# Routing in a two-layer encoder: picks moved behind a copy, a store on another queue, and turned identities ahead of the experts

## The chip, the cores and the metric

The kernel runs on one core of one Trainium2 chip. The metric is the device time of one execution in microseconds (us). TensorE does the matrix products, VectorE and ScalarE the elementwise work, GpSimd gathers and scatters rows by index, and SyncE issues most DMAs.

## The reference

A trunk of two layers over 1024 tokens of width 1024. Each layer is a mixer with an output projection and a residual add, then an RMS norm and a mixture of experts with two-step routing: the best of 4 groups, then the best two of its 8 experts, so 32 experts in all. The change touches only how the routing is scheduled, and the first moments of the experts.

```python
def hier_moe(x, wg, bg, we, be, w1, w3, w2):
    ...
    g_logits = (xt @ wg).astype(f32) + bg.astype(f32)
    g_prob = jax.nn.softmax(g_logits, axis=-1)
    g_idx = jnp.argmax(g_logits, axis=-1)
    ...
    e_logits = jnp.take_along_axis(e_logits, g_idx[:, None, None], axis=1)[:, 0]
    top_p, top_e = lax.top_k(jax.nn.softmax(e_logits, axis=-1), TOP_K)
    top_p = top_p / jnp.sum(top_p, axis=-1, keepdims=True)
    ...
    def expert_block(args):
        xe, e = args
        hid = jax.nn.silu(xe @ w1[e]) * (xe @ w3[e])
        return hid @ w2[e]
...
for layer in range(DEPTH):
    ...
    x = x + y                      # y: mixer output @ w_out
    x = x + hier_moe(rms_norm(x, ffn_norm[layer]), ...)
```

## The kernel before

The program is written out by hand, engine by engine: each stage is a block in which every engine has its own list of instructions, and semaphores (`wait_ge`, `then_inc`) order them. At the end of a block all engines meet; the next block starts when the last one has arrived. Nothing is scheduled by a planner; the order on an engine is the order in the code.

**Products.** Each product of 32-bit numbers is split into a high and a rest part: three matmuls (lines 211 to 213) of 128x128 by 128x512 for each of the eight pieces `k` of the inner dimension.

**The routing stage** is `out_route` (line 702), called once per layer: `"0"` at about 630 to 772 us and `"1"` at about 1780 to 1934 us. It does the output projection, the residual add, the norm, the router and the lists of tokens for each expert. The loop goes over 8 tiles of 128 tokens. On TensorE, tile `j` is: `project(j, 0)` (24 matmuls, half the columns), the turning of the rows of tile `j - 1` (`turn_x`, line 893, eight transposes by a product with the identity), then `project(j, 1)`, in whose middle (`k == 4`) stand the scores of tile `j - 1` (`logits`, line 912, 16 matmuls of 36 columns). The turned rows are copied out of the accumulator by ScalarE (lower half, line 1023) and VectorE (upper half, `move`, line 1124), and the scores wait for both.

**VectorE** has for each tile: rests of the inputs (line 201), `add(j, 0)` (line 1130), `move(j - 1)`, `add(j, 1)`, the norm's scale (`scale_of`, lines 1136 and 1139), the normed rows `xn` (line 1290). Between them stand the picks: `pick_group` and `pick_experts` turn the scores of one or more tiles into the two chosen experts per token, in some 20 small instructions in a row, each waiting for the one ahead. Before, the picks of tiles 0 to 3 stand at the very start of tile 5's round, those of tiles 4 and 5 at the start of tile 7's, tile 6's is cut in two around the last add, and tile 7's follows at the end. `early_slots` (lines 1235 to 1251) turns picks into places in the experts' lists, from sums that TensorE makes (`early_places`, lines 920 and 924).

**The end of the stage** is a chain: the last pick, `mark_slots` (1246 to 1251), TensorE's `list_slots` (line 941, a pair of matmuls per tile), the slots (line 1306), the gates (1309 to 1318), sixteen matmuls (line 979) and the copy of `slot_gate` (1330, 1331). SyncE stores the last normed rows to `xn_scratch` (line 832), behind two loads of 2 MB of expert weights each (line 179). GpSimd waits for the slots and for that store, and issues the gathers of the first two experts' rows (line 848).

**The experts' stage** is `experts` (line 1951). Per expert: three chunks of weights of 2 MB each, cast to a high part on ScalarE (line 2317) and a rest on VectorE (line 2381) in halves, and the products of lines 2193, 2195 and 2201 on TensorE. It opens on TensorE with `turn_x(0, 0, 0)` (line 2210), eight transposes of the gathered rows. ScalarE first casts one half chunk, then moves the turned rows; VectorE likewise. `idle_products(bank, n)` is an existing helper (line 203) that turns the identity `n` times into an unused bank; other stages open with 36, 30 and 44 of them.

## Time and profile before

| what | value |
|---|---|
| time, median of 3 runs | 2561.81 us (2560.67 to 2567.5) |
| the profiled execution's own time | 2555.0 us |
| its span | 2553.1 us |
| TensorE busy | 2394.8 us (94%) |
| VectorE busy | 1841.6 us (72%) |
| ScalarE busy | 1458.3 us (57%) |
| mean granted TensorE clock | 0.970 |
| routing stage of layer 0, of layer 1 | about 639 to 772, 1780 to 1934 us |

The page gives busy times by engine and, in 40 slices of the span, busy tenths, the granted clock of TensorE (1.0 is 2.4 GHz, 0.5 is 1.2 GHz) and the DMA engines' share. A timeline row is the start in us from the start of the span, the duration, the engine, the line of the kernel, what is written from what, the shape and the count; in square brackets stand the idle time ahead of it and what ended that. Rows of the same kind that follow one another are merged. Matmuls are pipelined, so a row's duration is longer than the distance to the next.

### The profile page before, as it was taken

Reading aid. Unit: us, or ns where it says so; the run is one execution under the profiler, and the core shown is the slowest. Engines: PE = TensorE matmul, PEld = TensorE weight load, DVE = VectorE, ACT = ScalarE, POOL = GpSimd, SP = SyncE. Lnnn points to the kernel's source line nnn. Section 1 sums busy time; section 2 is a strip of 40 time slices with the busy share of each in tenths; the row PEclk is TensorE's granted clock in tenths of the full one; section 3 lists DMA queues with packets and bytes.
Section 4 is the critical chain, followed back from the end, with each engine's and each line's share of the span. In section 5 each row is a group of like instructions: output and inputs, shape, how many; then the busy total and the mean of one; then the engine's idle time right before and its main releaser. Section 6 shows DMA issues by size and latency. Waiting matters only on the chain. (4 is left out here: it accounts for less than half of the span.)

```text
span 2553.1 us, 32636 instructions
## 1 busy us (share of the span) xinstructions
PE 2394.8 (94%) x11674; PEld 1966.4 (77%) x11674; DVE 1841.6 (72%) x2189; ACT 1458.3 (57%) x1782; POOL 478.3 (19%) x433
## 2 busy tenths in 40 slices
PE   8989999897998999999998999997997999999997
PEld 6768877576887888888886877875876888888884
DVE  6838855667468998898894241378668999898983
ACT  6437843321316878888783241267415788888872
POOL 0001100102001332333320000026001433332321
PEclk9999999999998999999998999999998999999999
DMA  5110002110337999999994022022427999999997
GB/s 183 34 67 1 1 17 70 75 34 9 126 134 272 374 393 383 389 383 380 381 379 158 17 105 94 33 50 84 155 80 274 369 385 377 369 397 379 394 378 278
DMA packets 93944, 540.19 MB, mean 212 GB/s; under 512 B 19212, under 2 KB 31085, under 8 KB 68246
## 3 DMA queue, kind: packets, MB, share of 16 engines
q1 hardware_dynamic: 72390, 500.81, 50.4%
q0 software_dynamic: 19008, 33.61, 5.5%
q10 hardware_dynamic: 2448, 4.46, 0.5%
q8 instruction: 62, 1.02, 0.2%
q14 instruction: 36, 0.29, 0.0%
HBM read 519.37 MB, written 55.08 MB: 225 GB/s over the span
## 5 line engine op out<-in xcount | busy, mean ns | idle before, releaser
L2381 DVE TENSOR_TENSOR wL_rest<-ring,wH 128x2048 fp32r<-128x2048 f32 x384 | 868.0, 2288 | 117.1 <-ACT wH L2317 111.1
L2317 ACT CAST wH<-ring 128x2048 fp32r<-128x2048 f32 x384 | 729.5, 1911 | 157.2 <-DMA ring<-in_moe_w 126.7
L2193 PE MATMUL psum<-wH,xgH 128*128 128x512 f32 x1024 | 407.5, 398 | 11.3 <-DVE xgL L2381 11.2
L2195 PE MATMUL psum<-wH,xgL 128*128 128x512 f32 x1024 | 401.1, 392 | 0.0
L2201 PE MATMUL psum<-wL_rest,xgH 128*128 128x512 f32 x1024 | 275.1, 391 | 0.0
L2193 PEld LDWEIGHTS psum<-wH,xgH 128*128 128x128 f32 x1024 | 193.4, 189 | 52.9 <-DVE xgL L2381 13.6
L2201 PEld LDWEIGHTS psum<-wL_rest,xgH 128*128 128x128 f32 x1024 | 192.9, 188 | 40.6
L2195 PEld LDWEIGHTS psum<-wH,xgL 128*128 128x128 f32 x1024 | 193.7, 189 | 38.3
L2193 PE MATMUL psum<-wH,hidH 128*128 128x512 f32 x512 | 206.0, 402 | 3.9 <-DVE hidL L2381 3.9
L2195 PE MATMUL psum<-wH,hidL 128*128 128x512 f32 x512 | 200.2, 391 | 0.0
L2110 POOL COPY gidx<-slots 128x1 int32 (+1 forms) x60 | 61.5, 1025 | 495.6 <-PE psum L2210 495.6
L2201 PE MATMUL psum<-wL_rest,hidH 128*128 128x512 f32 x512 | 137.7, 391 | 0.0
L213 PE MATMUL psum<-xn_high,ring_rest 128*128 128x512 f32 x320 | 126.6, 396 | 0.0
L2193 PEld LDWEIGHTS psum<-wH,hidH 128*128 128x128 f32 x512 | 96.5, 189 | 23.2 <-DVE hidL L2381 4.4
L211 PE MATMUL psum<-w_high_route_rest,y_high_route 128*128 128x512 f32 x256 | 105.4, 412 | 9.3 <-DVE ring_rest L201 8.7
L2201 PEld LDWEIGHTS psum<-wL_rest,hidH 128*128 128x128 f32 x512 | 96.7, 189 | 20.2
L2195 PEld LDWEIGHTS psum<-wH,hidL 128*128 128x128 f32 x512 | 96.7, 189 | 18.3
L2124 POOL COPY yidx<-slots 128x1 int32 (+1 forms) x64 | 97.0, 1516 | 58.0 <-DMA out<-y,yidx 37.9
L213 PE MATMUL psum<-w_high_route_rest,y_rest_route 128*128 128x512 f32 x256 | 101.7, 397 | 0.0
L212 PE MATMUL psum<-ring_rest,y_high_route 128*128 128x512 f32 x256 | 101.2, 395 | 0.0
L2328 ACT ACTIVATE y<-psum,slot_gate 128x1024 f32<-128x1024 f32 x64 | 71.4, 1116 | 51.8 <-PE psum L2201 51.2
L212 PE MATMUL psum<-ring_rest,xn_high 128*128 128x512 f32 x256 | 100.3, 392 | 0.0
(453 smaller groups left out, 4672.5 us busy)
## 6 DMA issues: line engine op xcount, KB each, us to landing
ring<-in_moe_w SPq DMA_DIRECT2D x192, 2048.0 KB
ring<-in_ev_w_in SPq DMA_DIRECT2D x6, 2048.0 KB
ring<-in_od_w_in SPq DMA_DIRECT2D x6, 2048.0 KB
xn_scratch<-xn_route SPq DMA_DIRECT2D x16, 512.0 KB, 2.7
xnT<-in_moe_w SPq DMA_DIRECT2D x4, 2048.0 KB, 12.8
v_att<-in_x SPq DMA_DIRECT2D x8, 512.0 KB, 4.1
ring<-in_ev_w_out SPq DMA_DIRECT2D x2, 2048.0 KB
xnT<-in_x SPq DMA_DIRECT2D x8, 512.0 KB, 3.7
```

Of the source, the lines that this page charges most:

```text
L211: nc.tensor.matmul(dst, lhs[0], rhs[0], start=start, stop=False)
L212: nc.tensor.matmul(dst, lhs[0], rhs[1], start=False, stop=False)
L213: return nc.tensor.matmul(dst, lhs[1], rhs[0], start=False, stop=stop)
L2110: nc.gpsimd.tensor_copy(idx[:, b:b + 1], slots[:, bass.ds(e, 1)]).then_inc(idx_ok, 1)
L2124: nc.gpsimd.tensor_copy(yidx[:, b:b + 1], slots[:, bass.ds(e, 1)]).then_inc(yidx_ok, 1)
L2193: nc.tensor.matmul(psum[:, bank, :], xh[:, k, :], w3[0][:, n, cols], start=(half == 0 and n == 0), stop=False)
L2195: nc.tensor.matmul(psum[:, bank, :], xl[:, k, :], w3[0][:, n, cols], start=False, stop=False)
L2201: ins = nc.tensor.matmul(psum[:, bank, :], xh[:, k, :], w3[1][:, n, cols], start=False, stop=(half == 1 and n == len(ks) - 1))
L2317: nc.scalar.copy(half_of(wH, b, e, c, half), raw(e, c, half)).then_inc(w_high, 1)
L2328: nc.scalar.activation(y[:, b, :], psum[:, 5:7, :].rearrange("p a b -> p (a b)"), ACT.Copy, scale=slot_gate[:, bass.ds(e, 1)]).then_inc(y_ ...
L2381: return nc.vector.tensor_tensor(out, whole, high.bitcast(F32), ALU.subtract)
```

## The change

On **VectorE** the picks of tiles 0 to 3 stand behind `add(5, 0)` and `move(4)`; tile 4's pick stands behind the early lists in tile 6's round; tile 5's opens tile 7's round; tile 6's is whole and stands ahead of the last add. On **TensorE** the scores of tiles 4 and later each wait for a read by the pick three picks back; in the last tile the early sums and tile 6's scores stand at `k == 2`, no longer at 4; the list products of tiles 0 to 3 are put between the two halves of the last turn; the totals (line 973) stand behind the last pair of list products. On **ScalarE** the last `move` stands ahead of the last square, and ScalarE stores the last normed rows from its own queue, ahead of the exponential; SyncE no longer does. In the experts' stage TensorE turns the identity 20 times ahead of `turn_x(0, 0, 0)` and 12 times behind it. No arithmetic of the result changes.

```diff
@@ SyncE
-                            sp.wait_ge(xn_ok, j + 1)
-                            sp.dma_start(xn_d[j * P:(j + 1) * P, :], xn[:, j % 2, :]).then_inc(xn_out[j % 2], 16)
+                            if j < NT - 1:
+                                sp.wait_ge(xn_ok, j + 1)
+                                sp.dma_start(xn_d[j * P:(j + 1) * P, :], xn[:, j % 2, :]).then_inc(xn_out[j % 2], 16)
@@ TensorE, project
-                                if c == 1 and k == 4:
-                                    if j == 7:
+                                if c == 1 and k == (2 if j == NT - 1 else 4) and j:
+                                    if j == NT - 1:
                                         early_places(1)
...
@@ TensorE, logits
-                                if j == 4:
-                                    pe.wait_ge(logit_read, 1)
                                 if j == 5:
                                     pe.wait_ge(places_read, 1)
-                                if j == 6:
-                                    pe.wait_ge(logit_read, 2)
-                                if j == 7:
-                                    pe.wait_ge(logit_read, 3)
+                                if j >= 4:
+                                    pe.wait_ge(logit_read, j - 3)
@@ TensorE, end of the stage
                         turn_x(NT - 1, 0)
+                        pe.wait_ge(marked, 1)
+                        list_slots(0, 4)
                         turn_x(NT - 1, 1)
...
-                        list_slots(0, 6)
+                        list_slots(4, 6)
                         places(7, 0)
                         pe.wait_ge(marked, 3)
                         list_slots(6, 7)
-                        pe.wait_ge(places_read, 3)
+                        pe.wait_ge(marked, 4)
+                        list_slots(7, 8).then_inc(listed, 1)
                         for j in range(NT):
                             last = nc.tensor.matmul(psum[:, 1, 0:NE], onesR[:], both[:, j, :], start=(j == 0), stop=(j == NT - 1))
                         last.then_inc(totalled, 1)
-                        pe.wait_ge(marked, 4)
-                        list_slots(7, 8).then_inc(listed, 1)
@@ ScalarE
+                            if j == NT - 1:
+                                move(j)
                             act.wait_ge(added, 2 * j + 2)
...
-                            if j == NT - 1:
-                                move(j)
...
+                        act.wait_ge(xn_ok, NT)
+                        nc.scalar.dma_start(xn_d[(NT - 1) * P:NT * P, :], xn[:, (NT - 1) % 2, :]
+                                            ).then_inc(xn_out[(NT - 1) % 2], 16)
@@ VectorE
                         for j in range(NT):
-                            if j == 5:
-                                pick_group(slice(0, 4))
-                                pick_experts(slice(0, 4))
                             if j == 7:
-                                pick_group(slice(4, 6))
-                                pick_experts(slice(4, 6))
+                                pick(slice(5, 6))
...
                             if j:
                                 move(j - 1)
+                            if j == 5:
+                                pick(slice(0, 4))
                             if j == 6:
...
                                 early_slots(0)
+                                pick(slice(4, 5))
                             if j == 7:
                                 early_slots(1)
-                                pick_group(slice(6, 7))
+                                pick(slice(6, 7))
                             add(j, 1)
...
-                                pick_experts(slice(6, 7))
@@ experts, TensorE
+                        idle_products(OB, 20)
                         turn_x(0, 0, 0)
+                        idle_products(OB, 12)
```

`pick(js)` is `pick_group(js)` followed by `pick_experts(js)`. `early_places` and `places` wait for the picks by their new count.

On VectorE at tile 5 of layer 0, before (L1231 is the last instruction of the picks of tiles 0 to 3, L1124 the copy of the turned rows, L1130 an add):

```order
L1189 TENSOR_TENSOR chosen<-idx_route,mk_route 128x128
L1231 TENSOR_TENSOR both_route<-chosen 128x128
L201 TENSOR_TENSOR y_rest_route<-yT,y_high_route 128x512 x2
L1130 TENSOR_TENSOR xnT<-xnT,psum 128x512
L1124 COPY xnT<-psum 128x512
L1130 TENSOR_TENSOR xnT<-xnT,psum 128x512
```

and in the change:

```order
L201 TENSOR_TENSOR y_rest_route<-yT,y_high_route 128x512 x2
L1130 TENSOR_TENSOR xnT<-xnT,psum 128x512
L1124 COPY xnT<-psum 128x512
L1202 TENSOR_TENSOR logits_route<-psum,rs_route 128x144
L1207 TENSOR_TENSOR logits_route<-logits_route,b_route 128x144
L1209 TENSOR_REDUCE gm_route<-logits_route 128x4
```

The copy L1124 stood behind the picks and now stands ahead of them; the picks (from L1202 on) now have the second add behind them.

On TensorE at the end of the routing stage of layer 0, before (L893 turns a half of the last rows, L941 lists, L973 totals, L979 weighs; phase_sem1_41 is `marked`, phase_sem1_38 `picked`, phase_sem1_47 `places_read`):

```order
L893 MATMUL psum<-ident,xnT 128x128 [waits phase_sem1_3,phase_sem1_16,phase_sem1_15]
L893 MATMUL psum<-ident,xnT 128x128 x3
L893 MATMUL psum<-ident,xnT 128x128 [waits phase_sem1_3]
L893 MATMUL psum<-ident,xnT 128x128 x3
...
L941 MATMUL psum<-tok_of_route,xnT_rest 128x32 [waits phase_sem1_41]
L941 MATMUL psum<-tok_of_route,xnT_rest 128x32
L973 MATMUL psum<-both_route,ones_route 128x32 [waits phase_sem1_47]
L973 MATMUL psum<-both_route,ones_route 128x32 x7
L941 MATMUL psum<-tok_of_route,xnT_rest 128x32 [waits phase_sem1_41]
L941 MATMUL psum<-tok_of_route,xnT_rest 128x32
L979 MATMUL psum<-w_high_route_rest,xnT_rest 128x64 [waits phase_sem1_40]
```

and in the change (L937 lists, L931 places, L972 totals, L976 weighs):

```order
L893 MATMUL psum<-ident,xnT 128x128 [waits phase_sem1_3,phase_sem1_16,phase_sem1_15]
L893 MATMUL psum<-ident,xnT 128x128 x3
L937 MATMUL psum<-tok_of_route,xnT_rest 128x32 [waits phase_sem1_41]
L937 MATMUL psum<-tok_of_route,xnT_rest 128x32 x7
L893 MATMUL psum<-ident,xnT 128x128 [waits phase_sem1_3]
L893 MATMUL psum<-ident,xnT 128x128 x3
...
L931 MATMUL psum<-both_route,upper_route 128x32 [waits phase_sem1_38]
L937 MATMUL psum<-tok_of_route,xnT_rest 128x32 [waits phase_sem1_41]
L937 MATMUL psum<-tok_of_route,xnT_rest 128x32
L937 MATMUL psum<-tok_of_route,xnT_rest 128x32 [waits phase_sem1_41]
L937 MATMUL psum<-tok_of_route,xnT_rest 128x32
L972 MATMUL psum<-both_route,ones_route 128x32 x8
L976 MATMUL psum<-w_high_route_rest,xnT_rest 128x64 [waits phase_sem1_40]
```

Eight list products now stand between the halves of the turn, and the totals behind the last pair of lists.

On TensorE at the start of the experts of layer 0, before (L2210 turns the gathered rows, L2193 is the first product):

```order
L792 UNCONDITIONAL_BRANCH
L2184 UNCONDITIONAL_BRANCH [waits barrier_Pool_Activation_PE_DVE_SP_release]
L2210 MATMUL psum<-ident,xg 128x128 [waits gather_in0]
L2210 MATMUL psum<-ident,xg 128x128 x7
L2193 MATMUL psum<-wH,xgH 128x512 [waits phase_sem0_5,phase_sem0_4]
```

and in the change (L206 turns the identity, L2211 the gathered rows, L2194 is the first product):

```order
L792 UNCONDITIONAL_BRANCH
L2185 UNCONDITIONAL_BRANCH [waits barrier_Pool_Activation_PE_DVE_SP_release]
L206 MATMUL psum<-ident 128x128 x20
L2211 MATMUL psum<-ident,xg 128x128 [waits gather_in0]
L2211 MATMUL psum<-ident,xg 128x128 x7
L206 MATMUL psum<-ident 128x128 x12
L2194 MATMUL psum<-wH,xgH 128x512 [waits phase_sem0_5,phase_sem0_4]
```

The identity is turned 20 times ahead of the wait for the gather and 12 times ahead of the first product.

## Rows read from the trace of the kernel before

**Rows 1.** Timeline, VectorE and TensorE at tile 5 of both layers (start us, us, engine).

```profile
710.72 0.30 DVE L1202 TENSOR_TENSOR logits_route<-psum,rs_route 128x144 f32<-128x144 f32 x1
...
716.75 1.29 DVE L201 TENSOR_TENSOR y_rest_route<-yT,y_high_route 128x512 fp32r<-128x512 f32 x2
...
719.29 1.08 PE L912 MATMUL psum<-w_gain_route,xnT 128*128 128x36 f32 x8 [2.47 <-DVE xnT L1124]
...
1878.04 1.43 PE L912 MATMUL psum<-w_gain_route,x_turned_route 128*128 128x36 f32 x8 [3.67 <-DVE x_turned_route L1124]
```

**Rows 2.** Timeline at tile 6 of both layers, same columns.

```profile
731.42 1.22 DVE L1251 TENSOR_TENSOR xnT_rest<-place_of,cst 128x1024 fp32r<-128x1024 f32 x1
...
732.57 1.87 PE L912 MATMUL psum<-w_gain_route,xnT 128*128 128x36 f32 x16
...
1893.68 1.23 DVE L1251 TENSOR_TENSOR xnT_rest<-place_of,cst 128x1024 fp32r<-128x1024 f32 x1
...
1893.83 1.87 PE L912 MATMUL psum<-w_gain_route,x_turned_route 128*128 128x36 f32 x16
```

**Rows 3.** Timeline of layer 0 from the last product of the stage.

```profile
751.48 0.60 PE L893 MATMUL psum<-ident,xnT 128*128 128x128 f32 x4
...
757.52 0.26 DVE L1199 SCALAR_TENSOR_TENSOR logits_route<-psum,rs_route,b_route 128x36 f32<-128x36 f32 x1 [0.19 <-PE psum L912]
...
761.29 0.22 DVE L1235 TENSOR_TENSOR tok_of_route<-chosen,tok 128x64 fp32r<-128x64 f32 x1
...
762.78 0.43 DVE L1251 TENSOR_TENSOR xnT_rest<-place_of,cst 128x256 fp32r<-128x256 f32 x1
...
765.19 0.19 DVE L1306 TENSOR_SCALAR slots<-psum 128x32 int32<-128x32 f32 x1 [1.68 <-PE psum L941]
...
771.93 0.19 DVE L1331 TENSOR_TENSOR slot_gate<-slot_gate,psum 128x32 f32<-128x32 f32 x1
```

**Rows 4.** Timeline of layer 1 at the same places.

```profile
1913.15 0.60 PE L893 MATMUL psum<-ident,x_res_route 128*128 128x128 f32 x4
...
1918.92 0.25 DVE L1199 SCALAR_TENSOR_TENSOR logits_route<-psum,rs_route,b_route 128x36 f32<-128x36 f32 x1
...
1934.15 1.90 ACT L2317 CAST wH<-ring 128x2048 fp32r<-128x2048 f32 x1 [8.97 <-PEq L792]
```

**Rows 5.** Chain of waits at the end of layer 1 (start us, us, what).

```profile
1919.03 12.80 DMA xn_scratch<-xn_route
...
1932.90 3.77 DMA xg<-xn_scratch,slots
```

**Rows 6.** DMA issues of the whole span (KB each, median us to landing).

```profile
sigmoid_o_scratch<-ml_sigmoid_o ACTq DMA_DIRECT2D x16, 256.0 KB, 2.0
...
xg<-xn_scratch,oidx POOLq DMA_INDIRECT x3, 6.8
```

**Rows 7.** Timeline, head of layer 0's experts, then layer 1's second expert.

```profile
772.47 1.90 ACT L2317 CAST wH<-ring 128x2048 fp32r<-128x2048 f32 x1 [8.69 <-PEq L792]
...
772.90 1.97 PE L2210 MATMUL psum<-ident,xg 128*128 128x128 f32 x8 [1.24 <-DMA xg<-xn_scratch,slots]
777.95 0.79 PE L2193 MATMUL psum<-wH,xgH 128*128 128x512 f32 x1 [3.08 <-DVE xgL L2381]
...
783.10 0.40 PE L2193 MATMUL psum<-wH,xgH 128*128 128x512 f32 x1
...
788.55 2.29 DVE L2381 TENSOR_TENSOR wL_rest<-ring,wH 128x2048 fp32r<-128x2048 f32 x1 [2.35 <-ACT wH L2317]
...
793.89 0.50 PE L2193 MATMUL psum<-wH,xgH 128*128 128x512 f32 x1 [1.56 <-DVE xgL L2381]
...
1955.24 0.50 PE L2193 MATMUL psum<-wH,xgH 128*128 128x512 f32 x1 [1.56 <-DVE xgL L2381]
```

**Rows 8.** Windows: engines busy, PEclk, DMA share, GB/s; stage start and experts.

```profile
1364.00:1372.00 8.00, 7.52 (x44) 7.48 (x44) 3.50 (x5) 6.50 (x9) 0.00 (x0) 0.62 0.82 272
...
2060.00:2080.00 20.00, 20.00 (x98) 16.66 (x96) 18.14 (x12) 17.08 (x15) 6.21 (x5) 1.00 1.00 391
```

15 lines of the change are left out of this document (8 added, 7 removed).

## The prediction, made before the changed kernel was run

> **What bounds the kernel now.** I read the windows first, then the waits in order of time. In the experts' stages TensorE is busy 20.00 of 20.00 us at full clock and the DMA share is 1.00 [rows 8], so there nothing is idle and a microsecond won at the start of a stage moves everything behind it. The change touches the two routing stages and the start of the two experts' stages behind them; I write "tile" for 128 tokens, E for the moment at which TensorE starts to turn the last tile's rows (751.48 and 1913.15 [rows 3, 4]) and T for ScalarE's first cast of the experts' stage (772.47 and 1934.15 [rows 4, 7]). From S to T it is 20.99 and 21.00 us, and this stretch is a chain through VectorE: last picks, slots, gates, a last product. Inside the routing stage TensorE runs back to back but for one pause per layer, at tile 5: 2.47 and 3.67 us, both ended by VectorE's copy of the turned rows [rows 1]. In the timeline the reader is to see why: VectorE begins the picks of tiles 0 to 3 at 710.72 and reaches its next other work at 716.75 [rows 1], 6.03 us in which the copy waits.
>
> **Step 1, the picks of tiles 0 to 3 behind the copy.** TensorE's pause goes: -2.47 and -3.67. What is late next is VectorE's second add of tile 5. With the copy done about 3.3 us after 710.72, the 6.03 us of picks end some 9.2 us behind it. That product ends a little under 13 us behind 710.72 before; less the pause, that leaves about 1 us of slack in layer 0, and 1.5 us by the same count in layer 1. I take nothing for it.
>
> **Step 2, the new wait.** The scores of tile 5 now wait until VectorE has read the scores of tile 4, and that read is queued behind the early marks. In layer 0 the marks end at 731.42 + 1.22 = 732.64 and TensorE comes at 732.57; with the read's 0.26 (the one-tile read in [rows 3]) and a hand-over that is 0.4 us. In layer 1 they end at 1893.68 + 1.23 = 1894.91 against TensorE at 1893.83 [rows 2]: 1.08 + 0.26 = 1.3 us. Both engines come earlier by the same pause, so the differences stand. Bounds: 0.3 to 0.6 and 1.2 to 1.6. Behind the waiting TensorE stand only its own products of tile 6. Splitting tiles 4 and 5 costs VectorE two picks of 761.29 - 757.52 = 3.77 us [rows 3] in place of one double, in its idle time under the products of tiles 6 and 7; the second ends just as TensorE asks for it, which may cost 0.1.
>
> **Step 3, the last pick starts sooner.** It starts 757.52 - 751.48 = 6.04 us behind S in layer 0 and 1918.92 - 1913.15 = 5.77 in layer 1 [rows 3, 4]. Ahead of it stood the second part of tile 6's pick, 10 of its 16 instructions, so 10/16 x 3.77 = 2.4 us; that is now over before the last add. Not all of it is won, since the copy then waits for the turned rows: eight list products stand between the two halves of the turn, 0.12 us each by the 16 in 1.87 of [rows 2], and TensorE stood idle for part of that already. Turn, copy, mean, root and scaling then follow one another, and I put the start at S + 4.7: -1.3 and -1.1. From 0 to -2.4, nearer the middle because both ends of the chain are known.
>
> **Step 4, the totals behind the lists.** VectorE waits 1.68 us for the lists [rows 3]. Its last mark is ready at 762.78 + 0.43 = 763.21, and the last pair of list products, at the slow clock 1.97 / 8 = 0.25 each [rows 7], needs 0.5; the eight totals stood ahead of them. Without those the slots come 1.3 us sooner: -1.3 per layer (-1.0 to -1.4). The totals fall into TensorE's wait for the gates, and nobody waits for them.
>
> **Step 5, the store from ScalarE's queue.** In layer 1 the last normed rows take 12.80 us to land behind 4 MB of weights on SyncE's queue, and the gather behind them 3.77 [rows 5]. On ScalarE's own queue it can take 2.0 us, the quiet price for half the size, or 6.8, a gather's price while weights stream [rows 6], or still 12.80. ScalarE has nothing to do there but wait for the exponential's input, so the issue costs nothing. I take 6.8: issued at S + 4.6, landed by S + 11.5, when the slots are there too (S + 11.1). Then GpSimd no longer ends the stage; VectorE's chain does, and -0.3 more falls to layer 1, where T came later behind it. The Trainium skill (DMA: Bandwidth & Descriptors, Queues, rings and completion order) has each DMA engine take turns between the queues packet by packet, which speaks for the middle price; no row here shows two such queues at once.
>
> **Sum up to T.** Layer 0: -2.5 + 0.4 - 1.3 - 1.3 = -4.7. Layer 1: -3.7 + 1.3 - 1.1 - 1.3 - 0.3 = -5.1.
>
> **Step 6, the turned identities.** Before, the first twelve products ran from 777.95 to 783.10, 5.15 us, 0.43 us each. The 98 matmuls in 20 us of [rows 8], one in seven of them a short turn, come to 0.22 to 0.23 us for a long one, 2.7 us for twelve: 2.4 us is what the risen clock is worth. The price: 20 turns at the slow clock are at most 20 x 0.25 = 4.9 us by the eight in 1.97 [rows 7], and about 4.3 since the last one's full length is in those 1.97; only then come the eight of x. Turned identities do bring the clock up in this trace: the stage that begins before 1372 opens with 44 of them and nothing else, busy 7.52 of the 8 us from 1364.00, so from 1364.48; the mean granted clock over these 8 us is 0.62 [rows 8], that is 6.1 us at the lower level (1.2 GHz) and the rest at 2.4 GHz, a rise 5.5 us after the first turn. The long products after 777.95 had it within about 5 us (0.79 us for the first, 0.40 at 783.10 [rows 7]). If it rises 4 us behind T, x is turned by T + 5.3 in place of T + 2.4, ScalarE's casts of the weights behind it come 3 us late, and the first product starts at T + 6.8 in place of 777.95 - 772.47 = 5.5, but warm. The first twelve are then over at T + 9.5 in place of T + 10.6. VectorE has 2.35 us of idle time at 788.55 [rows 7] to take up ScalarE's lateness. The second expert starts at T + 20.4 in place of 793.89 - 772.47 = 21.4 in layer 0 and of 1955.24 - 1934.15 = 21.1 in layer 1: -1.0 and -0.7. Bounds: a rise at 5.5 us leaves -0.5 and -0.2, one at 3 us gives -1.8 and -1.5; with the clock up at T already it would be -2.4 each. Weights follow VectorE's casts and land well ahead of their use at the head.
>
> **Total.** -4.7 - 5.1 - 1.0 - 0.7 = -11.5. The profiled execution is 2555.0 us (span 2553.1); the median of the three timed runs is 2561.81, 6.8 above. So 2543.5 in the profile's terms and 2550.3 as a median; I forecast **2550.3**. Its own range, by the bounds above and the 2 us by which runs differ, is 2546 to 2555.
>
> **Rivals.**
> *A, the identities don't raise the clock.* Then 20 turns, eight of x and twelve more stand in a row at the slow clock: first product at T + 8.9, first twelve as slow as before, second expert 3.4 and 3.7 us later than now: -9.8 + 7.1 = -2.7, **2559.1**. Against it speaks the rise at 1364.48 + 5.5 under turned identities alone. The Trainium skill (TensorE: Matmul & The Clock Gate, Part 4: PE-mode transpose) says that the full clock "doesn't engage" for transposes; by that rule A holds, and this trace disagrees with it, with 0.62 over a stretch that holds only turns.
> *B, the store stays late.* If the weights, issued first, still hold it back 11 to 13 us, the gathers start at S + 16 to S + 18 and T is 0.5 and 1.6 later than in my sum; the rows still land ahead of the turned identities' end. -9.4, **2552.4**. For it: all 16 DMA engines are shared; against it: 6.8 for a gather among the same loads.
> *C, slower than before.* The store and the gathers go on ending the stage, so that T stays at S + 21.0 and only the pauses are won (-2.1 and -2.4), and the turned identities then stand in the chain at the slow clock with their whole 7.1: -4.5 + 7.1 = +2.6, **2564.4**. It decides at a landing later than S + 18; before it was 1931.83 - 1913.15 = 18.7 (12.80 behind 1919.03 [rows 5]). Both conditions are needed, and each has a row against it.
> *D, the clock is up early.* If what TensorE does at the end of routing counts too, or the rise comes within 3 us, the head gives up to 4.8 in place of 1.7: **2547.2**. Against it: the same small products left it slow before, through the turns of x at 0.25 us each [rows 7].
> *E, the stall of step 1 reappears.* The picks delay an add that TensorE needs; up to 2 us per layer back: **2554.3**.
>
> **How the numbers follow.** Forecast 0.55, A 0.08, B 0.15, C 0.04, D 0.10, E 0.08. The range goes from D's 2547 less noise to A's 2559: 2545 to 2559; C and the outer part of D stay out. 0.3%, about what a measurement of this kernel can tell from no change, is 7.7 us: faster means under 2554.1. That holds for the forecast but its upper edge, for D, most of B and half of E: 0.75. A, the rest of B and E, and most of C are within: 0.22. Slower by that much needs more than C: 0.03.
>
> **What would show it.** Step 1: the pauses of 2.47 and 3.67 before TensorE's scores at tile 5 are gone. Step 2: short idle times of about 0.4 and 1.3 before its scores at tile 6. Steps 3 and 4: the last pick at S + 4.7 and slots at S + 11.1, from 13.7 before. Step 5: a landing of 5 to 8 us and gathers right behind the slots. Sum: T at S + 18.3. Step 6: granted clock 1.00 from the first product on and the second expert at T + 20.4. Wrong if T stays at S + 21, if the first products take 0.43 us each, or if the experts' stage stretches by what its start won.

## The result, and the profile after

The changed kernel takes 2546.97 us (median of 8 runs, 2543.09 to 2550.17) against 2562.28 us (8 runs, 2554.51 to 2567.5) for the kernel before, measured beside it. The ratio is 0.9940, with a 95% interval of 0.9926 to 0.9954: faster by 15.3 us, 0.6%, clear of the noise. The prediction said 2550.3 with a range of 2545 to 2559, so the median lies 3.3 us below the forecast and inside the range. (Where the prediction introduces "E for the moment at which TensorE starts to turn the last tile's rows", it means the S that all its sums use; so do the texts below.)

The profiled execution took 2544.74 us (span 2542.7), 10.3 us less than the profiled one of before. So the medians differ by 5 us more than the profiles do, and that is the first question for the experiments.

Timeline of the changed kernel at tiles 5 and 6 of both layers (start us, us, engine, line, what, count, idle time ahead). It answers [rows 1, 2]:

```profile
715.84 1.87 PE L908 MATMUL psum<-w_gain_route,xnT 128*128 128x36 f32 x16
...
730.25 1.95 PE L908 MATMUL psum<-w_gain_route,xnT 128*128 128x36 f32 x16 [0.18 <-issue]
...
1867.31 1.87 PE L908 MATMUL psum<-w_gain_route,x_turned_route 128*128 128x36 f32 x16
...
1883.64 1.95 PE L908 MATMUL psum<-w_gain_route,x_turned_route 128*128 128x36 f32 x16 [1.18 <-issue]
```

At tile 5 the 16 products for the scores follow without a pause, in both layers. At tile 6 the new wait stands where step 2 put it. The row prints 0.18 us of it in layer 0; by the distance between two turns of x the tile costs 0.42 more than before (14.49 in place of 14.07). In layer 1 it is 1.18 us.

Timeline from the last turn of x to ScalarE's first cast, against [rows 3, 4]: last turn, last pick, slots, product for the gates, the two gathers, slot gates, then the same two ends in layer 1.

```profile
749.39 0.60 PE L893 MATMUL psum<-ident,xnT 128*128 128x128 f32 x4
...
753.83 0.26 DVE L1199 SCALAR_TENSOR_TENSOR logits_route<-psum,rs_route,b_route 128x36 f32<-128x36 f32 x1
...
760.22 0.19 DVE L1307 TENSOR_SCALAR slots<-psum 128x32 int32<-128x32 f32 x1 [0.39 <-PE psum L937]
...
763.08 3.62 PE L976 MATMUL psum<-w_high_route_rest,xnT_rest 128*128 128x64 f32 x16 [1.19 <-DVE w_high_route_rest L1319]
...
765.70 1.23 POOL L849 DMA_INDIRECT xg<-xn_scratch,slots  x1 [128.47 <-issue]
767.22 1.00 POOL L849 DMA_INDIRECT xg<-xn_scratch,slots  x1 [0.30 <-issue]
...
766.96 0.19 DVE L1332 TENSOR_TENSOR slot_gate<-slot_gate,psum 128x32 f32<-128x32 f32 x1
...
1904.58 0.60 PE L893 MATMUL psum<-ident,x_res_route 128*128 128x128 f32 x4
...
1922.68 1.90 ACT L2320 CAST wH<-ring 128x2048 fp32r<-128x2048 f32 x1 [7.40 <-PEq L792]
```

The last pick starts at S + 4.44, the slots at S + 10.83, the slot gates 0.35 us ahead of T. T is 767.50 = S + 18.11, and in layer 1 S + 18.10 (20.99 and 21.00 before). VectorE's wait for the lists fell from 1.68 to 0.39 us. One thing did not happen: the gathers go out at S + 16.3, not at S + 11, because the store on ScalarE's queue still lands late.

Head of the experts' stage on TensorE, against [rows 7]:

```profile
767.54 4.50 PE L206 MATMUL psum<-ident 128*128 128x128 f32 x20 [0.84 <-PEq L792]
771.83 1.66 PE L2211 MATMUL psum<-ident,xg 128*128 128x128 f32 x8
773.32 1.47 PE L206 MATMUL psum<-ident 128*128 128x128 f32 x12
774.89 0.50 PE L2194 MATMUL psum<-wH,xgH 128*128 128x512 f32 x1
...
788.53 0.50 PE L2194 MATMUL psum<-wH,xgH 128*128 128x512 f32 x1 [1.60 <-DVE xgL L2384]
...
1943.11 0.50 PE L2194 MATMUL psum<-wH,xgH 128*128 128x512 f32 x1 [1.56 <-DVE xgL L2384]
```

The second expert starts at T + 21.03 in layer 0 and T + 20.43 in layer 1, in place of 21.42 and 21.09.

### The profile page after: what moved, and what is told of

Its sections match the earlier page's. It is cut to its first block and busy times, and to the rows that moved or that the text cites. A ratio compares the mean times of both kernels' runs of the same rounds, so it can differ in the third digit from the quotient of the medians.

```text
span 2542.7 us, 32784 instructions
## 1 busy us (share of the span) xinstructions
PE 2399.4 (94%) x11738; PEld 1972.5 (78%) x11738; DVE 1847.5 (73%) x2211; ACT 1461.0 (57%) x1782; POOL 491.3 (19%) x433
## 5 line engine op out<-in xcount | busy, mean ns | idle before, releaser
L2194 PE MATMUL psum<-wH,xgH 128*128 128x512 f32 x1024 | 405.7, 396 | 7.0 <-DVE xgL L2384 6.7
L2194 PEld LDWEIGHTS psum<-wH,xgH 128*128 128x128 f32 x1024 | 192.6, 188 | 47.2 <-DVE xgL L2384 8.9
L2194 PE MATMUL psum<-wH,hidH 128*128 128x512 f32 x512 | 206.0, 402 | 3.9 <-DVE hidL L2384 3.9
L2111 POOL COPY gidx<-slots 128x1 int32 (+1 forms) x60 | 70.5, 1174 | 497.0 <-PE psum L2211 497.0
L2125 POOL COPY yidx<-slots 128x1 int32 (+1 forms) x64 | 111.0, 1735 | 52.7 <-DMA out<-y,yidx 27.2
L2194 PEld LDWEIGHTS psum<-wH,hidH 128*128 128x128 f32 x512 | 96.5, 189 | 23.2 <-DVE hidL L2384 4.4
```

The source lines that it names most:

```text
L2111: nc.gpsimd.tensor_copy(idx[:, b:b + 1], slots[:, bass.ds(e, 1)]).then_inc(idx_ok, 1)
L2125: nc.gpsimd.tensor_copy(yidx[:, b:b + 1], slots[:, bass.ds(e, 1)]).then_inc(yidx_ok, 1)
L2194: nc.tensor.matmul(psum[:, bank, :], xh[:, k, :], w3[0][:, n, cols], start=(half == 0 and n == 0), stop=False)
```

## The experiments

Twelve runs were made: the kernel before once more, and eleven variants. The table holds what their timelines show. "Tile 5" and "tile 6" are the distances from one first turn of x (the row with ident as input and xnT or x_res, x8) to the next, layer 0 / layer 1; T - S, the first weights load behind T and the second expert behind T are read as above. "Lost" is what the experts from the fifth on took above 17.70 us each, from one turn of gathered rows to the next, summed over a stage. Medians are in us; the ratio is to runs of the kernel before on the same chip. These runs were spread over several chips, on which the kernel before had medians of 2560.6 to 2562.7, so two variants are better compared by their ratios.

| kernel | tile 5 | tile 6 | T - S | first load | second expert | lost | median (runs) | ratio to before |
|---|---|---|---|---|---|---|---|---|
| before, first profile | 16.26 / 20.01 | 14.07 / 14.57 | 20.99 / 21.00 | 7.65 / 9.31 | 21.42 / 21.09 | 0.3 / 1.3 | 2562.28 (8) | |
| before, second profile | 19.11 / 21.59 | 14.09 / 14.59 | 20.71 / 21.20 | 7.65 / 9.18 | 20.43 / 21.74 | 0.1 / 3.7 | 2560.06 (8) | 0.9997 |
| picks03 | 13.64 / 14.56 | 14.09 / 14.57 | 20.71 / 21.02 | 7.65 / 9.24 | 21.91 / 22.25 | 1.8 / 6.3 | 2551.77 (6) | 0.9959 |
| changed | 13.61 / 14.56 | 14.49 / 17.52 | 18.11 / 18.10 | 10.76 / 10.09 | 21.03 / 20.43 | 0.5 / 0 | 2546.97 (8) | 0.9940 |
| picks_old | 19.50 / 19.97 | 14.07 / 14.57 | 19.42 / 19.42 | 9.78 / 10.26 | 20.16 / 20.65 | 0.6 / 7.5 | 2557.92 (12) | 0.9987 |
| totals_ahead | 13.64 / 14.56 | 14.47 / 15.97 | 19.38 / 19.38 | 10.19 / 10.88 | 20.52 / 21.14 | 0.3 / 6.5 | 2547.05 (4) | 0.9944 |
| store_sync | 13.64 / 14.56 | 14.47 / 15.95 | 19.62 / 20.22 | 10.07 / 9.97 | 20.44 / 20.33 | 1.7 / 1.1 | 2549.25 (5) | 0.9957 |
| no_ident | 13.61 / 14.56 | 14.48 / 15.97 | 18.11 / 18.11 | 8.25 / 8.90 | 20.55 / 21.43 | 0.7 / 0.3 | 2546.75 (5) | 0.9942 |
| cast_first | 13.61 / 14.56 | 14.47 / 17.51 | 18.11 / 18.12 | 6.46 / 6.45 | 21.32 / 21.34 | 2.2 / 0.9 | 2546.52 (6) | 0.9932 |
| loads_same | 13.61 / 14.56 | 14.47 / 15.98 | 18.11 / 18.11 | 10.62 / 9.96 | 21.00 / 20.35 | 3.0 / 2.4 | 2545.59 (4) | 0.9931 |
| fill | 13.61 / 14.56 | 14.49 / 17.53 | 19.22 / 20.74 | 10.26 / 10.27 | 20.60 / 20.60 | 0 / 1.6 | 2546.82 (5) | 0.9941 |
| best1 | 13.61 / 14.56 | 14.07 / 14.57 | 18.64 / 18.54 | 9.38 / 9.25 | 21.18 / 21.21 | 1.8 / 2.5 | 2547.74 (6) | 0.9954 |
| best0 | 13.61 / 14.56 | 14.07 / 14.57 | 18.67 / 18.10 | 10.70 / 10.05 | 20.98 / 20.40 | 2.9 / 1.8 | 2543.79 (6) | 0.9932 |
| best2 | 13.61 / 14.56 | 14.07 / 14.57 | 18.37 / 17.91 | 10.65 / 9.86 | 21.00 / 20.22 | 0.2 / 4.1 | 2544.40 (6) | 0.9929 |

The intervals of the ratios are 0.001 to 0.002 to either side, 3 to 5 us. What lies within that of the changed kernel's 0.9940 is told apart by the timelines alone, and the last column says no more than "about the same".

### before_again: was the first profile typical?

> The kernel before, unchanged, profiled a second time. What is asked: whether the profile on which the prediction rests was a typical execution. Theory (a pause of TensorE is sometimes followed by a stretch at a granted clock of 0.50 and sometimes not, so the same pause has two prices): tile 5 of layer 0, from one first turn of x to the next, takes 16.26 us again or about 19.5, and in layer 1 20.0 again or 18.2; everything else up to S is as in the first profile within 0.1 us. Rival (the first profile was typical and the 5 us by which the medians differ more than the profiles lie in the experts' stages): both tiles as in the first profile, 16.26 and 20.01, and the experts' stages differ by more than 2 us.

Measured: 2564.55 us in the profiled execution, where the first one of before took 2555.0. Timeline of TensorE, the turns of x of tiles 4 and 5 and the products behind the pause between them; then windows of 2 us (us, busy time of PE, PEld, DVE, ACT and POOL, the granted clock, the DMA share, GB/s):

```profile
711.16 1.04 PE L893 MATMUL psum<-ident,xnT 128*128 128x128 f32 x8
...
718.21 1.92 PE L912 MATMUL psum<-w_gain_route,xnT 128*128 128x36 f32 x8 [2.43 <-DVE xnT L1124]
...
730.27 1.03 PE L893 MATMUL psum<-ident,xnT 128*128 128x128 f32 x8
...
717.00:719.00 2.00, 0.80 (x4) 0.80 (x4) 1.15 (x2) 0.00 (x0) 0.00 (x0) 0.61 0.00 0
719.00:721.00 2.00, 2.00 (x9) 1.81 (x9) 0.00 (x0) 0.00 (x0) 0.00 (x0) 0.50 0.03 8
721.00:723.00 2.00, 2.00 (x6) 1.58 (x5) 0.00 (x0) 0.00 (x0) 0.00 (x0) 0.50 0.00 0
723.00:725.00 2.00, 2.00 (x7) 1.55 (x6) 0.01 (x1) 0.00 (x0) 0.00 (x0) 0.68 0.00 0
```

and the same windows in the first profile of before:

```profile
719.00:721.00 2.00, 1.71 (x12) 1.58 (x13) 0.23 (x1) 0.00 (x0) 0.00 (x0) 1.00 0.04 8
721.00:723.00 2.00, 2.00 (x10) 1.66 (x9) 0.00 (x0) 0.00 (x0) 0.00 (x0) 1.00 0.00 0
```

The same pause, 2.43 us in place of 2.47, cost 5.50 us here (19.11 against the 13.61 of a tile without it) and 2.65 in the first profile. The difference is the granted clock: it fell to 0.50, the 1.2 GHz level, as TensorE stood idle, and TensorE then worked for some 6 us at that level, busy 2.00 of 2.00 us. Six microseconds at half speed lose 3, and 2.4 + 3 is nearly the whole 5.5. In the first profile it stayed at 1.00. In layer 1 the pause of 3.67 us cost 5.45 the first time and 7.03 the second. The theory holds for layer 0; for layer 1 neither expectation had 21.59.

The two profiles of before differ by 9.6 us in all, and tile 5 of both layers is 4.4 of them. Another 3.5 lie ahead of, between and behind the stages that the change touches (-1.1, 2.8 and 1.8), and 1.7 in the experts' stages (-1.3 and 3.0). So the rival is wrong on the tiles and right in part on the rest: the price of the pause is the largest single item of the difference between two executions, not the whole.

### picks03: step 1 alone

```diff
                         for j in range(NT):
-                            if j == 5:
-                                pick_group(slice(0, 4))
-                                pick_experts(slice(0, 4))
...
                                 move(j - 1)
+                            if j == 5:
+                                pick_group(slice(0, 4))
+                                pick_experts(slice(0, 4))
```

> The kernel before with step 1 alone: the picks of tiles 0 to 3 stand behind the copy of the turned rows at tile 5, all else as before. Theory (the pause and the stretch of slow clock behind it are most of the gain): tile 5 takes 13.61 and 14.56 us in place of 16.26 (19.5 with the slow stretch) and 20.01, from the first turn to S 91.1 and 96.2 us, T at S + 21.0 as before; the time is 8 to 11 us below the kernel before's median. Rival (step 1 is worth its two pauses, 2.47 + 3.67, or VectorE's second add of tile 5 is late instead): 4 to 6 us below.

Measured: 2551.77 us against 2560.87, ratio 0.9959 (0.9946 to 0.9973): 9.1 us by the medians and 10.5 by the ratio, from moving one step of VectorE behind one copy. Tiles and S are as the theory said (S 91.10 and 96.22 us behind the first turn), T - S as before.

### picks_old: all but the picks

The picks and TensorE's waits for them stand as before; everything else is the changed kernel. (The edit is the part of the diff on picks, logits and places, backwards.)

> The changed kernel with steps 1 to 3 undone: the picks stand where they stood before (0 to 3 ahead of tile 5's adds, 4 and 5 together ahead of tile 7, tile 6's pick split around the last add), and so do TensorE's waits for them; the list of tiles 0 to 3 between the two halves of the turn, the order of totals and lists, the store and the turned identities stay as changed. Theory (steps 1 to 3 as on record, plus what the clock adds: in layer 1 the pause of 3.67 us is followed by a stretch at a granted clock of 0.50): from the first turn of tile 0 to S 93.7 us in layer 0 and 101.7 in layer 1, where the changed kernel has 91.66 and 99.16; the last pick starts 6.0 and 5.8 us behind S, T comes at S + 19.4. Sum 2.1 + 2.5 + 1.3 + 1.3 = 7.2 us above the changed kernel's time, 8.7 where that one was spared the dip at tile 6. Rival (the gain of the picks is found again elsewhere, the rest of the change carries it): under 4 us above.

Measured: 2557.92 us, 11 above the changed kernel (12 by the ratios); expected were 7.2 to 8.7, by the rival under 4. T - S grew by 1.3 in both layers, as step 3 had it. Tile 5 of layer 0 took more than expected. Its pause on TensorE:

```profile
719.11 1.70 PE L913 MATMUL psum<-w_gain_route,xnT 128*128 128x36 f32 x8 [2.48 <-DVE xnT L1129]
```

The pause is 2.48 us, and between the turns around it lie 19.50: the price with the slow stretch, a second time. Between the two profiles 2.6 us are at the tail; up to S this profile is 5.3 us longer in layer 0 than the changed kernel's and 2.5 in layer 1 (4.0 against the profiles without the slow stretch at tile 6).

### totals_ahead: step 4 undone

```diff
-                        pe.wait_ge(marked, 4)
-                        list_slots(7, 8).then_inc(listed, 1)
+                        pe.wait_ge(places_read, 3)
                         for j in range(NT):
...
                         last.then_inc(totalled, 1)
+                        pe.wait_ge(marked, 4)
+                        list_slots(7, 8).then_inc(listed, 1)
```

> The changed kernel with step 4 undone: the eight totals stand ahead of the last list products. Theory: VectorE waits 1.7 us for the lists in place of 0.39, slots and T come 1.3 us later in each layer (T at S + 19.4), the time is 2.6 us above the changed kernel's. Rival (GpSimd, whose gathers went out only at S + 16.3 and S + 16.8, ends the stage anyway or the product for the gates does): T at S + 18.1 to S + 18.5 and no difference in time over 1 us.

Measured: T at S + 19.38 in both layers, 1.27 later than in the changed kernel, which is step 4 as predicted. Its median of 2547.05 is 0.1 above the changed kernel's, from four runs that range from 2543.22 to 2551.66: the time neither confirms nor refutes 2.6 us.

### store_sync: step 5 undone

```diff
-                            if j < NT - 1:
-                                sp.wait_ge(xn_ok, j + 1)
-                                sp.dma_start(xn_d[j * P:(j + 1) * P, :], xn[:, j % 2, :]).then_inc(xn_out[j % 2], 16)
+                            sp.wait_ge(xn_ok, j + 1)
+                            sp.dma_start(xn_d[j * P:(j + 1) * P, :], xn[:, j % 2, :]).then_inc(xn_out[j % 2], 16)
...
-                        act.wait_ge(xn_ok, NT)
-                        nc.scalar.dma_start(xn_d[(NT - 1) * P:NT * P, :], xn[:, (NT - 1) % 2, :]
-                                            ).then_inc(xn_out[(NT - 1) % 2], 16)
```

> The changed kernel with step 5 undone: the last normed rows are stored from SyncE's queue, behind the 4 MB of weights. Theory (the store is late on either queue, so the queue is worth what VectorE's chain leaves uncovered): the store lands 11 to 13 us behind its issue in place of 10.7 and 11.3, the gathers go out 0 to 1.5 us later, T stays at S + 18.1 in layer 0 and comes up to 1.2 us later in layer 1, 0 to 1.2 us in all. Rival (the store on ScalarE's queue is what lets VectorE's chain end the stage): T at S + 19.5 or later in both layers and 3 us or more in all.

Measured: the store lands 13.4 and 13.8 us behind its issue, T comes at S + 19.62 and S + 20.22, 1.5 and 2.1 us later; the median is 2.3 above the changed kernel's. The rival holds by the marks (3.6 us in both layers; 4.4 by the ratios). With VectorE's chain shortened to S + 18.1, the store on SyncE's queue ends the stage, so its move is worth 3.6 us in this kernel, and not the 0.3 of the prediction. Without it, steps 3 and 4 leave only 1.4 and 0.8 us of the 2.9 per layer.

### loads_same: the store beside the loads, not behind them

```diff
                             if j == NT - 1:
+                                sp.wait_ge(xn_ok, NT)
                                 for c in range(2):
```

> The changed kernel, but the two chunks of weights (4 MB) that are issued at the start of the last tile's turn wait until the last rows are normed, so they are issued at S + 4.5, at the same moment as the store on ScalarE's queue. Theory 1 (the store was held up by the 4 MB issued ahead of it, in the DMA engines themselves): with both issued together the store lands in 2.5 to 5 us in place of 10.7 and 11.3, and the first gather goes out right behind the slots, at S + 11, in place of S + 16.3 and S + 16.8. Theory 2 (the two queues share the engines for as long as both have work, whatever came first): the store still needs 6.8 us or more. For the time: if VectorE's chain ends the routing stage, T stays at S + 18.1 and the time within 1 us of the changed kernel's; if GpSimd's gathers end it, T falls to S + 17 or less.

Measured: issued at the same moment (751.07 and 751.06 us), the store lands in 9.0 and 9.2 us. Theory 2 holds. T stays at S + 18.11 although the gathers go out at S + 14.6 and S + 14.7: VectorE's chain ends the stage in the changed kernel, as the sum had it. This run also shows the price of tile 6 in layer 1 at its other value. First the changed kernel, windows behind its new wait of 1.18 us, which ends at 1883.64 (fields as above):

```profile
1884.00:1886.00 2.00, 2.00 (x17) 1.92 (x17) 1.70 (x9) 0.00 (x0) 0.00 (x0) 0.96 0.00 0
1886.00:1888.00 2.00, 2.00 (x6) 1.55 (x5) 0.99 (x5) 0.00 (x0) 0.00 (x0) 0.50 0.00 0
1888.00:1890.00 2.00, 2.00 (x8) 1.54 (x8) 0.00 (x0) 0.00 (x0) 0.00 (x0) 0.69 0.00 0
```

and loads_same, the row with the same wait and the windows behind it:

```profile
1885.65 1.95 PE L909 MATMUL psum<-w_gain_route,x_turned_route 128*128 128x36 f32 x16 [1.18 <-issue]
...
1886.00:1888.00 2.00, 2.00 (x18) 1.91 (x18) 1.69 (x9) 0.00 (x0) 0.00 (x0) 1.00 0.00 0
1888.00:1890.00 2.00, 2.00 (x10) 1.65 (x9) 1.01 (x5) 0.00 (x0) 0.00 (x0) 1.00 0.00 0
```

The same idle time of 1.18 us, the same work; in one execution TensorE fell to 0.50 behind it and the tile took 17.52 us, in the other it stayed at 1.00 and the tile took 15.98. (By the windows the stretch at 0.50 lasted 3.3 us, of which half, 1.6, is the difference.) Three of the seven kernels with this wait show about 17.5 (changed, cast_first, fill), four show about 16.0.

### no_ident: the head without turned identities

```diff
-                        idle_products(OB, 20)
                         turn_x(0, 0, 0)
-                        idle_products(OB, 12)
```

> The changed kernel without its turned identities (neither the 20 nor the 12); all else stays. Theory of step 6 (the identities raise the clock and what they cost is less than what they give): the first twelve long products take 0.43 us each again, the granted clock is 0.50 until about T + 10, the second expert starts at T + 21.0 to T + 21.4 as before, where the changed kernel had T + 21.03 and T + 20.43, so the time is 0.4 to 1.7 us above the changed kernel's. Rival (the identities only delay the turn of x, ScalarE's casts and with them the first weights load, and give back later what the clock won): the first weights load starts at T + 7.7 to T + 9.3 in place of T + 10.8 and T + 10.1, the third expert of layer 1 takes 19.5 us in place of 21.53, and the time is 1 to 3 us below the changed kernel's.

Measured: 2546.75 us, no difference from 2546.97. The second expert of both layers on TensorE, and the windows in which the granted clock rose (fields as above):

```profile
786.33 0.50 PE L2194 MATMUL psum<-wH,xgH 128*128 128x512 f32 x1 [1.56 <-DVE xgL L2382]
...
1942.46 0.50 PE L2194 MATMUL psum<-wH,xgH 128*128 128x512 f32 x1 [1.56 <-DVE xgL L2382]
...
774.00:776.00 2.00, 2.00 (x9) 1.64 (x8) 2.00 (x2) 1.98 (x2) 0.00 (x0) 0.91 0.66 133
...
1931.00:1933.00 2.00, 2.00 (x9) 1.65 (x8) 2.00 (x2) 1.46 (x2) 0.00 (x0) 0.88 0.76 221
```

T is 765.78 and 1921.03, so the second expert starts at T + 20.55 and T + 21.43: 0.5 us sooner than with the identities in layer 0, 1.0 us later in layer 1. Neither theory has both signs. The clock did what step 6 said: without identities it rises 8.6 and 10.4 us behind T, in the changed kernel 5.6 and 4.1. What that is worth is not settled. Over all profiles, the 16 heads with identities as changed average T + 20.6 (20.16 to 21.14), and the eight heads without (before twice, picks03, no_ident) T + 21.35 (20.43 to 22.25), 0.7 us later; but six of these eight belong to kernels whose end of routing also differs. The two of no_ident alone average T + 20.99, against 20.70 in changed and loads_same: 0.3 us. And where the rows of the 32nd expert are turned, the 16 are at T + 550.3 and T + 552.6 on average and the eight at T + 550.2 and T + 553.0, so a gain is not seen at the end of the stage. The first weights load starts 2.5 and 1.2 us sooner without identities, and the third expert of layer 1 takes 19.51 us, both as the rival said; but most kernels with identities have 19.5 there too, and the time is no shorter.

### cast_first: is the first weights load the next bound?

The changed kernel with the two halves of the first weights cast ahead of x, for the first expert only, on ScalarE and in the same way on VectorE:

```diff
                             split(b, e, 0, 0)
-                            move_x(e)
-                            split(b, e, 0, 1)
+                            if first(e):
+                                split(b, e, 0, 1)
+                                move_x(e)
+                            else:
+                                move_x(e)
+                                split(b, e, 0, 1)
                             split(b, e, 1, 0)
```

> The changed kernel, but in the first expert both halves of the first weights are cast before x is moved, on ScalarE and on VectorE. It fills the wait of 3.5 us for the turned x on ScalarE. Theory (behind the head the weights' loads are the next bound, and they wait for VectorE's pass over the first chunk): the first load starts at T + 6 to T + 7 in place of T + 10.8 and T + 10.1, the first product at T + 7.5 to T + 8, the second expert at T + 20.4 to T + 21.4, ScalarE's wait for the ring at the third expert falls from 2.95 and 4.66 us to under 1.5, layer 1's third expert takes 19.5 us or less in place of 21.53, and the time is 1 to 4 us below the changed kernel's. Rival (the stall of the third expert is an accident, and VectorE's own work sets the head): the loads start earlier but no product does, the second expert is up to 0.5 us later, and the time is the same or up to 1 us longer.

Why it was tried: in the changed kernel's layer 1 the third expert took 21.53 us, where the other profiles have 19.5. Rows of ScalarE and TensorE there, and the window behind:

```profile
1956.87 1.91 ACT L2320 CAST wH<-ring 128x2048 fp32r<-128x2048 f32 x1 [4.66 <-DMA ring<-in_moe_w]
...
1963.02 0.50 PE L2194 MATMUL psum<-wH,xgH 128*128 128x512 f32 x1 [1.90 <-DVE xgL L2384]
...
1965.00:1967.00 2.00, 2.00 (x6) 1.52 (x5) 2.00 (x2) 1.57 (x1) 1.27 (x1) 0.50 0.65 139
```

ScalarE waits 4.66 us for weights, TensorE then stands idle for 1.90 us (1.47 before), and its clock is 0.50 behind that. And cast_first, layer 1 (two casts, SyncE's first load, second expert, ScalarE's longest wait for the ring):

```profile
1924.12 3.70 ACT L2320 CAST wH<-ring 128x2048 fp32r<-128x2048 f32 x2 [7.41 <-PEq L792]
...
1930.58 6.31 SPq L2057 DMA_DIRECT2D ring<-in_moe_w  x2
...
1945.46 0.50 PE L2194 MATMUL psum<-wH,xgH 128*128 128x512 f32 x1 [1.56 <-DVE xgL L2388]
...
1956.80 1.91 ACT L2320 CAST wH<-ring 128x2048 fp32r<-128x2048 f32 x1 [2.23 <-DMA ring<-in_moe_w]
```

The load starts at T + 6.46 in place of T + 10.09, and the longest wait falls from 4.66 to 2.23 us; the theory had 1.5. But the second expert starts at T + 21.34, not sooner, the third takes 19.49 as in most profiles, and the time is 2546.52. The rival holds in the main: the load is earlier and no product is. The second expert still waits 1.56 us for VectorE's xgL, so the head is probably bound by VectorE's work on weights and x; no run took that work away. The late load cost something only where TensorE's idle time grew and the clock fell behind it: best0 waited 4.55 us for weights, TensorE stood idle for 1.83 and the third expert took 21.46; best2 waited 4.30, with 1.55 idle and 19.55. Changed and best0 are two of the 16 stages with identities as changed; none of the eight without has it.

### fill and best1: can the clock be held through the end of routing?

fill adds 20 turned identities behind list_slots(4, 6), where TensorE waits for the last pick, and 12 behind the totals, where it waits for the gates' factors.

> The changed kernel with more turned identities in two waits of TensorE at the end of routing: 20 while it waits for the last pick (idle 2.74 and 2.4 us) and 12 while it waits for the gates' factors (idle 1.19 us). Theory (turned identities count for the clock wherever they stand, and narrow products run at half speed only because of the idle time between them): the granted clock stays at 1.00 through the end of routing, the 16 products for the gates take 1.9 us in place of 3.62, T comes at S + 16.0 to S + 17.0 in place of S + 18.1, and the 20 identities of the head take 2.3 us in place of 4.5: first product at T + 5.5, second expert at T + 19.5. The time is 3 to 6 us below the changed kernel's. Rival (narrow products let the clock fall whatever stands between them, or GpSimd's late gathers then end the stage): the clock is 0.50 at T again, or T stays at S + 17.5 or more, and the time is within 1.5 us of the changed kernel's.

Timeline of TensorE and two windows:

```profile
754.38 2.40 PE L206 MATMUL psum<-ident 128*128 128x128 f32 x20
757.27 0.28 PE L931 MATMUL psum<-both_route,upper_route 128*128 128x32 f32 x1 [0.49 <-DVE both_route L1233]
...
759.11 0.61 PE L937 MATMUL psum<-tok_of_route,xnT_rest 128*128 128x32 f32 x2 [0.45 <-DVE xnT_rest L1257]
...
761.26 2.82 PE L206 MATMUL psum<-ident 128*128 128x128 f32 x12
763.74 3.60 PE L978 MATMUL psum<-w_high_route_rest,xnT_rest 128*128 128x64 f32 x16
...
757.00:759.00 2.00, 0.68 (x3) 0.49 (x3) 1.84 (x9) 0.00 (x0) 0.00 (x0) 0.99 0.90 367
759.00:761.00 2.00, 1.89 (x9) 1.89 (x10) 1.40 (x10) 0.24 (x1) 0.00 (x0) 0.50 1.09 463
```

In layer 0 the 20 run at full clock (0.12 us each), and the clock falls about 2 us behind them, amid narrow products with idle times of 0.45 to 0.70 us. In layer 1 they run at the slow level already, 4.53 us in all. The 12 then run at the slow level (0.24 us each), are not done when the factors are, and the gates' product takes 3.60 us as ever. T comes 1.1 and 2.6 us later; the median does not show it. The rival holds.

best1 takes more identities, and two edits more:

```diff
+                                sp.wait_ge(xn_out[(NT - 1) % 2], 16 * (NT // 2))
                                 for c in range(2):
...
                         list_slots(4, 6)
+                        idle_products(6, 24)
                         places(7, 0)
+                        idle_products(6, 5)
                         pe.wait_ge(marked, 3)
                         list_slots(6, 7)
+                        idle_products(6, 3)
...
                         last.then_inc(totalled, 1)
+                        idle_products(6, 16)
                         pe.wait_ge(factors, 1)
...
+                                dve.wait_ge(placed, 1)
+                                read_scores(slice(4, 5))
                                 early_slots(0)
-                                pick(slice(4, 5))
+                                pick(slice(4, 5), False)
...
-                        idle_products(OB, 20)
+                        idle_products(OB, 8)
                         turn_x(0, 0, 0)
-                        idle_products(OB, 12)
+                        idle_products(OB, 20)
```

(read_scores is the first instruction of the pick, with its signal.)

> The changed kernel with three edits that can be read apart. (a) VectorE reads the scores of tile 4 ahead of the early marks, so TensorE's new wait at tile 6 (0.18 and 1.18 us) should be gone: first turn to S 91.4 us in layer 0 and 96.4 in layer 1 (the dip of the clock that followed the wait in some executions, 1.54 us, gone too), in place of 91.66 and 97.62 or 99.16. (b) The last 4 MB of weights wait until the last normed rows have landed: the store lands in 2 to 4 us, in place of 10.7 and 11.3, and the gathers go out at S + 11. If it still needs 9 us with nothing beside it, no other queue was the cause. (c) Turned identities in every wait of TensorE from the last pick on (24, 5, 3 and 16), 8 ahead of the turn of x and 20 behind it. Theory (a gap of a few tenths of a microsecond was what let the clock fall behind the 20 of the last experiment): the clock stays at 1.00, the product for the gates takes 1.9 us, T comes at S + 16.3, the second expert at T + 19.5 or sooner, and the time is 4 to 8 us below the changed kernel's. Rival (narrow products let the clock fall whatever fills the gaps): the 16 identities ahead of the gates' product run at the slow clock and push T to S + 20, and with the 28 of the head the time is 0 to 4 us above what (a) alone would give.

Measured: (a) holds. The first turn to S takes 91.24 and 96.21 us, and the wait at tile 6 is gone in both layers. (b) With nothing beside it the store lands in 2.6 and 3.3 us; the gathers go out at S + 14, since the slots came late too. (c) is half true. TensorE in layer 0:

```profile
752.36 5.38 PE L206 MATMUL psum<-ident 128*128 128x128 f32 x24
...
762.14 1.97 PE L981 MATMUL psum<-w_high_route_rest,xnT_rest 128*128 128x64 f32 x16 [0.23 <-DVE w_high_route_rest L1330]
764.95 1.94 PE L206 MATMUL psum<-ident 128*128 128x128 f32 x8 [0.84 <-PEq L792]
```

Here the clock was low before the identities began, and 24 of them took 5.38 us in a wait that is 2.74 us long in the changed kernel: the slots are 2 us late, at S + 12.9. But they brought the clock up, and the gates' product took 1.97 us in place of 3.62. In sum T came at S + 18.64 and S + 18.54, 0.5 and 0.4 us later than in the changed kernel. At the head the clock was low once more, behind a product of 64 columns and an idle time of 0.84 us. The median, 2547.74, is the changed kernel's.

### best0 and best2: what seemed worth keeping

best0 is the changed kernel with edit (a) and with only the second of the two loads held until the store has landed; best2 adds 12, 4, 2 and 8 identities at the four places of best1, and keeps 20 and 12 at the head.

> The changed kernel with the scores of tile 4 read ahead of the early marks, and the second of the last two weights' loads held until the last normed rows have landed. Theory: first turn to S 91.2 and 96.2 us (97.62 or 99.16 in the changed kernel), the store lands in 3 to 5 us in place of 10.7 and 11.3, the gathers go out at S + 11 to S + 12, T stays at S + 18.1 since VectorE's chain ends it, and the time is 2 to 3 us below the changed kernel's. Rival (the later load makes the experts' second and third weights late): ScalarE waits for the ring by over 3 us at the second or third expert, and the time is that of the changed kernel or longer.

> The kernel of the last run with turned identities in TensorE's waits at the end of routing as well, half as many ahead of the last pick's product as in the earlier trial: 12, 4, 2, and 8 ahead of the gates' product; 20 and 12 at the head as in the changed kernel. Theory (24 in a wait of 2.7 us were too many at the slow clock, where one takes 0.22 us; 12 fit it at either clock): the slots come at S + 10.8 to S + 11.2, the gates' product takes 2.0 us in place of 3.62, T comes at S + 16.5 to S + 17, the time is 2 to 3 us below the last run's. Rival (12 do not bring the clock up in time): the gates' product takes 3.6 us and T comes at S + 18.1 to S + 18.8, the time is that of the last run or up to 1 us longer.

Measured: best0 takes 2543.79 us (2541.26 to 2548.69), best2 2544.40 (2537.85 to 2548.9). Both beat the kernel before clearly. Their medians are 3.2 and 2.6 us below the changed kernel's (2.0 and 2.8 by the ratios), with ranges that overlap its 2543.09 to 2550.17, so that they beat it too is not shown. What is shown is the wait at tile 6: 14.07 and 14.57 us in every profile with edit (a), against 14.47 and 15.95 to 17.53. The store lands in 7.4 and 8.2 us, so the theory's 3 to 5 was wrong, and the gathers go out at S + 13.0 and S + 13.7, not by S + 12; T came at S + 18.67 and S + 18.10. (In layer 0 of best0 the last pick started 0.56 us later than elsewhere, at S + 5.00.) best0's rival was right in one point, the wait of 4.55 us for weights in layer 1. In best2 the gates' product took 3.60 and 3.05 us: 12 identities do not bring the clock up in time, and the rival holds: T came at S + 18.37 and S + 17.91.

The store's landing in five kernels, each value from "DMA to landing" of its line. The changed kernel's page has the price for 512 KB in quiet (median 2.6), and its own two stores:

```profile
xn_scratch<-xn_route SPq DMA_DIRECT2D x14, 512.0 KB, 2.6
...
L1069 ACTq DMA_DIRECT2D xn_scratch<-xn_route x2: 326/330/334, 753.9 to 1909.0; - x2
...
DMA to landing us min/median/max: 10.7/11.0/11.3
```

| what stands ahead of or beside the 512 KB | landing, us |
|---|---|
| nothing (best1) | 2.6, 3.3 |
| 2 MB issued about 3 us earlier on SyncE's queue, 2 MB held (best0) | 7.4, 8.2 |
| 4 MB issued at the same moment on SyncE's queue (loads_same) | 9.0, 9.2 |
| 4 MB issued about 3 us earlier on SyncE's queue (changed) | 10.7, 11.3 |
| the same 4 MB, store on the same queue (store_sync) | 13.4, 13.8 |

The four other kernels whose store stands as in the changed one (picks_old, totals_ahead, no_ident, cast_first) land it in 10.3 to 11.3 us, and fill in 11.5 and 11.9. In the kernel before, with the store on SyncE's queue but issued some 4.5 us behind the 4 MB, not 3.2, it took 10.9 us in layer 0 and 12.8 in layer 1: a queue of its own is worth 2.5 to 2.7 us only at the same distance from the loads.

## Why the prediction was right, and where it was not

**What bounds.** Right. S and T were the right marks: tiles 0 to 4 take the same in all profiles within 0.03 us, and the experts go on at 17.70 us each.

**Step 1, the pauses.** The pauses went, as said, and no second add came late: in picks03 and in every later kernel but picks_old tile 5 takes what its neighbours take, 13.6 and 14.56 us. So rival E fell. The size was wrong. The step priced a pause at its idle time, 2.47 and 3.67 us; over the three profiles with the old picks it cost 2.65, 5.50 and 5.89 us in layer 0 and 5.45, 7.03 and 5.41 in layer 1, on average 4.7 and 6.0. The first profile, on which the prediction rests, happened to hold the cheapest of these prices in layer 0. Its layer 1 already held the answer: the tile was 5.45 us longer than its neighbours with a pause of 3.67, and the difference was never asked about.

**Step 2, the new wait.** 0.4 and 1.3 us were predicted. It costs 0.4 in layer 0. In layer 1 it costs 1.4 or 2.95 us, by whether the clock falls behind it, 2.1 on average over seven profiles.

**Step 3.** The last pick starts at S + 4.44 (4.7 predicted), and undoing the picks moves T by 1.3 us in both layers.

**Step 4.** 1.3 predicted, 1.27 measured. The slots came at S + 10.83 and S + 10.81.

**Step 5.** Wrong twice. The store does not land in 6.8 us but in 10.7 and 11.3, which is rival B's mechanism; a gather's price under load was the wrong row to be nearest to. And rival B's price for it, T 0.5 and 1.6 us later, was wrong too: the second gather goes out at S + 17.8 and S + 18.3, and with the gathers 1.7 and 2.1 us sooner T stays where it is (loads_same). The step's worth of 0.3 was undersized as well. It was counted against the old chain; against the new one it is 1.5 and 2.1 us (store_sync). The Trainium skill (DMA: Bandwidth & Descriptors, Queues, rings and completion order) has an engine change between queues packet by packet. The landings speak for some such sharing, since a queue of its own gains 2.5 to 2.7 us over the same queue; but it is no even sharing of bytes, by which the store issued beside 4 MB would land within twice its quiet 2.6 us, and it needs 9.0. No run shows the turns themselves.

**Sum up to T.** Predicted -4.7 and -5.1. In the two profiles: -2.07 - 2.88 = -4.95 and -2.49 - 2.90 = -5.39. This is where luck comes in: the pauses were priced by the one profile that held the cheap price, and measured against the same one. Rival C needed T to stay at S + 21.0; it fell to 18.1.

**Step 6.** Right on the clock; the worth is not shown. By the windows the clock rose 5.6 us behind T in layer 0 (0.73 over the 2 us from 772.00), the step's late bound, for which it had -0.5; the two profiles give -0.39. In layer 1 it rose 4.1 us behind T (0.80 over the 2 us from 1926.00), as the step assumed, with -0.7; the two profiles give -0.66. That both fit is luck, since the same mark differs by 1.0 and 0.65 us between the two profiles of before, and the comparison with no_ident gives 0.3 per layer. Rival A fell: with turned identities alone on TensorE from T on, the clock rose, and the last 12 of them run at 0.12 us each against 0.22 for the first. The Trainium skill's sentence that the full clock "doesn't engage" for transposes (TensorE: Matmul & The Clock Gate, Part 4: PE-mode transpose) does not hold for this kernel. Rival D fell as well: fill shows that narrow products at the end of routing do not hold the clock even with identities between them.

**The total.** The median lies inside the range, 3.3 us below the forecast. With the average prices of all profiles: tiles 5 and 6 give -4.7 + 0.4 - 6.0 + 2.1 = -8.2, T - S gives 18.11 - 20.94 = -2.8 per layer (20.94 being the mean of six stages of before and picks03), the head -0.7 per layer. That is -8.2 - 5.7 - 1.5 = -15.4 us, where the medians differ by 15.3. So close a match is luck: with 0.3 for the head it is -14.5, the price of the pause is an average of three values 3.2 us apart in layer 0, and the interval of the ratio alone is 3.6 us to either side. The prediction had -4.8, -5.3 and -1.7, less 11.5 in all. So it named the right places, with step 5's landing wrong and step 5's worth too small, and what it missed in size is step 1's and step 2's share of the slow clock. It also added the 6.8 us between profile and median of before as if they were a constant. They were the distance of one execution on the cheap side from a typical one, part of which the change then removed; after the change, profile and median are 2.2 us apart.

**What stays open.** The experts from the fifth on lose between 0 and 7.5 us per stage in single stalls, with no relation to the edits (column "lost"). This scatter hides edits of 1 to 3 us in a median of five runs, and its cause was not tried. The stretches that no edit touches scatter as well: over the fourteen profiles, from the 32nd expert of layer 0 to the first turn of x in layer 1 it is 487.4 to 491.6 us, and behind the 32nd expert of layer 1 67.8 to 70.6. Nor was it tried what decides in which execution the clock falls behind a given idle time.

## What to carry to other kernels

Price a short pause of TensorE not by its idle time but by the distance between two like marks around it, compared with neighbours that have none: 2.4 us idle cost 2.65 us once and 5.5 to 5.9 twice, 1.18 us cost 1.4 or 2.95. Here the one moved step of VectorE that had made TensorE wait gave 9 to 10.5 of the 15 us, and all the work on the tail and the head the rest. One profile can show the cheap price, and where the price depends on the execution, a second profile is needed. When two chains end a stage, count an edit to one of them against the length that the other will have after all edits, not the one it has now.

## What the runs showed of the hardware

- The granted clock fell from 1.00 to 0.50 around idle times of 1.18, 1.83, 1.90, 2.43 and 2.48 us (changed, best0, changed, before_again, picks_old) and stayed low for several microseconds of uninterrupted work. In other executions 1.18 us (loads_same) and 2.47 us (the first profile of before) passed at 1.00. Narrow products (32 columns) with gaps of 0.45 to 0.70 us between them did not hold it at 1.00, even behind 20 turned identities (fill).
- Turned identities alone raise it: in the changed kernel the first 20 take 0.22 us each and the last 12 take 0.12. Behind 24 and more of them in the waits of best1 the gates' product of 16 took 1.97 us in place of 3.62.
- A 512 KB store took 2.6 and 3.3 us alone (best1) and 9.0 to 11.9 us beside or behind 4 MB on another queue. A queue of its own was worth 2.5 to 2.7 us (store_sync against changed); keeping the large loads back was worth 8 (best1 against changed).
